# A two-layer decoder trunk on one core: two of seven activation blocks of the last MLP's down pairs kept in DRAM as high and low parts

## What is computed

```python
h = _modulate(_rmsnorm(x, norm_g[layer, 1]), sh2, sc2)
y = jnp.square(jax.nn.relu(h @ mlp_w_up[layer])) @ mlp_w_down[layer]
x = x + g2[:, None, :] * y
```

## Time and profile before

| | us |
|---|---|
| median of 3 runs | 2564.92 (2563.69 to 2565.44) |
| the profiled execution | 2562.76 |
| its span | 2561.0 |
| PE busy | 2484.8 (97%) |
| DVE busy | 1712.5 (67%) |
| ACT busy | 1041.6 (41%) |
| up pairs of the last MLP | about 1945 to 2212 of the span |
| down pairs | about 2258 to 2508 |
| last plain units | about 2511 to 2557 |

### The profile page before, as it was taken

How to read it: one execution, slowest core, us unless ns; L and a number is a source line. 1 busy time by engine, 2 the same in 40 slices (tenths; PEclk the granted TensorE clock), 3 DMA queues, 4 the chain that set the end, 5 groups by cost and what they waited for, 6 DMA issues and landing times. The chain is left out here.

```text
span 2561.0 us, 33801 instructions
## 1 busy us (share of the span) xinstructions
PE 2484.8 (97%) x12076; PEld 2028.1 (79%) x12076; DVE 1712.5 (67%) x2132; ACT 1041.6 (41%) x1486; POOL 149.1 (6%) x155
## 2 busy tenths in 40 slices
PE   6999999999999999999999999999999999998998
PEld 4888888888888878888898887666788888877877
DVE  6878776668876666666633545777259777588873
ACT  5553342236445431111311335777326544434321
POOL 0000000000000000000000003666000000000000
PEclk9999999999999999999999999999999999999999
DMA  6335573213444475553142364554333444734412
GB/s 256 128 136 185 192 261 117 99 58 125 163 160 152 172 272 187 186 206 135 48 151 75 112 176 136 127 128 107 123 115 107 144 158 149 270 113 151 175 43 111
DMA packets 135898, 378.54 MB, mean 148 GB/s; under 512 B 12656, under 2 KB 29040, under 8 KB 131824
## 3 DMA queue, kind: packets, MB, share of 16 engines
q1 hardware_dynamic: 135792, 377.11, 43.2%
HBM read 279.54 MB, written 97.52 MB: 147 GB/s over the span
## 5 line engine op out<-in xcount | busy, mean ns | idle before, releaser
L2435 PE MATMUL PS<-H_HI,W_HI 128*128 128x512 f32 x700 | 277.1, 396 | 3.3 <-DVE H_LO L1643 2.2
L2437 PE MATMUL PS<-H_HI,W_LO 128*128 128x512 f32 x700 | 272.9, 390 | 0.0
L2436 PE MATMUL PS<-H_LO,W_HI 128*128 128x512 f32 x700 | 272.6, 389 | 0.0
L2435 PE MATMUL PS<-HID_HI,W_HI 128*128 128x512 f32 x640 | 251.3, 393 | 7.2 <-DVE HID_LO L1869 3.3
L411 ACT ACTIVATE W_HI<-RAW 128x1024 fp32r<-128x1024 f32 x90 | 93.9, 1057 | 386.4 <-PE PS L2437 292.0
L2437 PE MATMUL PS<-HID_HI,W_LO 128*128 128x512 f32 x640 | 249.7, 390 | 0.0
L2436 PE MATMUL PS<-HID_LO,W_HI 128*128 128x512 f32 x640 | 249.7, 390 | 0.0
L1699 DVE SCALAR_TENSOR_TENSOR X<-PS,MODV,X 128x1024 f32<-128x1024 f32 x76 | 97.4, 1282 | 145.6 <-PE PS L2437 138.3
L2356 DVE TENSOR_TENSOR_SCAN KEEP<-PS,MASK 128x1024 f32<-128x1024 f32 (+3 forms) x112 | 147.6, 1349 | 46.9 <-ACT PS L1520 37.6
L2435 PEld LDWEIGHTS PS<-H_HI,W_HI 128*128 128x128 f32 x700 | 131.5, 188 | 32.9 <-DVE H_LO L1643 4.2
L2437 PEld LDWEIGHTS PS<-H_HI,W_LO 128*128 128x128 f32 x700 | 131.4, 188 | 28.3
(11 more groups left out here) (270 smaller groups left out, 5811.7 us busy)
## 6 DMA issues: line engine op xcount, KB each, us to landing
RAW<-in_wt SPq DMA_DIRECT2D x184, 512.0 KB, 4.1
MODRAW<-in_modw SPq DMA_DIRECT2D x96, 512.0 KB, 3.3
B_RAW<-block_scratch SPq DMA_DIRECT2D x21, 1024.0 KB, 8.0
hid_scratch<-TN SPq DMA_DIRECT2D x66, 256.0 KB, 2.2
HRAW<-hid_scratch SPq DMA_DIRECT2D x8, 2048.0 KB, 8.6
hid_scratch<-SCR SPq DMA_DIRECT2D x60, 256.0 KB, 2.2
x_scratch<-X SPq DMA_DIRECT2D x3, 4096.0 KB, 13.4
X<-x_scratch SPq DMA_DIRECT2D x6, 2048.0 KB, 8.7
```

The lines of the kernel that those rows point to most:

```text
L2435: pe.matmul(dst, w_hi, m_hi, start=first, stop=False)
L2436: pe.matmul(dst, w_hi, m_lo, start=False, stop=False)
L2437: return pe.matmul(dst, w_lo, m_hi, start=False, stop=last)
```

## The change

In the up pairs, N3 and N4 are cut as soon as their differences are made: ACT copies TD3 and TD4 into unused places of the weight ring (`down_hi`, before the first `finish` of the pair), DVE subtracts (`down_lo`, between the cut of S4 and `c12`), in place. SP stores four blocks for the two (`store_cut`, behind the first store of a pair), and N1 and N2 as before. The DRAM scratch has nine blocks a pair instead of seven. In the down pairs, `load_block` loads N3 and N4 twice, straight into B_HI and B_LO; their `b_hi` on ACT and `b_lo` on DVE are gone, and PE's product waits for the DMAs instead. In the last down pair DVE makes one of the four HID_LO before the addition of M22's bank and three behind it, where it made all four before. The diff, with the declarations of the new semaphores (`td_hi`, `td_lo`) and changes of counts left out where they only renumber:

```diff
@@ -37,7 +37,8 @@
...
 DPAIRS = 3 * GROUP_PAIRS
-M11, N1, N2, M21, N3, M22, N4 = range(PRODUCTS)
+M11, N1, N2, M21, N3, M22, N4, N3_HI, N4_HI = range(PRODUCTS + 2)
+CUT_HERE = PRODUCTS - 2
 W1, W2, WA, W3, W4, WD = range(BLOCKS)
...
@@ -298,6 +299,8 @@
...
                               enumerate((RC, RC + 2 * KB, RX + 28 * KB, RX + 30 * KB))]
+        TD3_HI, TD4_HI = W_HI[:, 4:8, 3 * P:4 * P], W_LO[:, 4:8, 3 * P:4 * P]
+        TD3_LO, TD4_LO = [at(f"TD_LO{n}", [P, HALF], F32R, off) for n, off in ((3, RC + 2 * KB), (4, RX + 30 * KB))]
         WX_HI = at("WX_HI", [P, 8, 3 * P], F32R, RX)
...
@@ -589,16 +592,22 @@
...
                 def store_sums(p, x):
-                    to = {n: BD[(p + DPAIRS * n).v] for n in (N1, N2, N3, N4)}
-                    made = [(p * 4 + n).v for n in range(1, 5)]
+                    to = {n: BD[(p + DPAIRS * n).v] for n in (N1, N2)}
+                    made = [(p * 4 + n).v for n in (1, 3)]
                     sp.wait_ge(sem["td_made"], made[0])
...
                     sp.wait_ge(sem["td_made"], made[1])
-                    sp.dma_start(to[N3], TD3[:]).then_inc(sem["td_out"], 16)
-                    sp.wait_ge(sem["td_made"], made[2])
                     sp.dma_start(to[N2], TD2[:]).then_inc(sem["td_out"], 16)
-                    sp.wait_ge(sem["td_made"], made[3])
-                    sp.dma_start(to[N4], TD4[:]).then_inc(sem["td_out"], 16)
+
+                def store_cut(p):
+                    to = {n: BD[(p + DPAIRS * n).v] for n in (N3_HI, N4_HI, N3, N4)}
+                    made = [(p * 2 + n).v for n in (1, 2)]
+                    sp.wait_ge(sem["td_lo"], made[0])
+                    sp.dma_start(fours(to[N3_HI]), TD3_HI.bitcast(F32)).then_inc(sem["td_out"], 16)
+                    sp.dma_start(to[N3], TD3_LO[:].bitcast(F32)).then_inc(sem["td_out"], 16)
+                    sp.wait_ge(sem["td_lo"], made[1])
+                    sp.dma_start(fours(to[N4_HI]), TD4_HI.bitcast(F32)).then_inc(sem["td_out"], 16)
+                    sp.dma_start(to[N4], TD4_LO[:].bitcast(F32)).then_inc(sem["td_out"], 16)
 
...
@@ -614,6 +623,8 @@
...
                         load_mod(sp, p // 2 * 3 + GMODS + 2)
+                    if sums:
+                        store_cut(p - 1)
                     store(p, 2, 0, 1, 1)
...
@@ -696,7 +707,12 @@
...
                     a = DPAIRS * b + GROUP_PAIRS * g
-                    sp.dma_start(B_RAW[b][:], BD[a:a + GROUP_PAIRS].rearrange("j p s -> p j s")
+                    if b in (N3, N4):
+                        h = DPAIRS * (N3_HI if b == N3 else N4_HI) + GROUP_PAIRS * g
+                        sp.dma_start(B_HI[b][:].bitcast(F32), BD[h:h + GROUP_PAIRS].rearrange("j p s -> p j s")
+                                     ).then_inc(sem[f"b_in{b}"], 16)
+                    to = B_LO[b][:].bitcast(F32) if b in (N3, N4) else B_RAW[b][:]
+                    sp.dma_start(to, BD[a:a + GROUP_PAIRS].rearrange("j p s -> p j s")
                                  ).then_inc(sem[f"b_in{b}"], 16)
...
@@ -720,7 +736,7 @@
...
                     sp.wait_ge(sem[f"hs_out{b}"], 64 * (PAIRS // 2) * 2 + 64 * 6)
-                sp.wait_ge(sem["td_out"], 16 * 3 * DPAIRS)
+                sp.wait_ge(sem["td_out"], 16 * 5 * DPAIRS)
                 sp.wait_ge(sem["product"], count_of(2, p, PRODUCTS, 7).v)
...
@@ -1218,6 +1234,8 @@
...
                         block_cut(p + 1, 1 - x, b)
+                    if m == 2 and (p.i is not None or p.c):
+                        down_hi(p - 1)
                     if stat:
...
@@ -1227,6 +1245,14 @@
...
                             act.activation(V_TOT[:], V_SPREAD, ACT.Copy).then_inc(sem["v_kept"], 1)
+
+                def down_hi(p):
+                    if p.i is not None or p.c:
+                        act.wait_ge(sem["td_out"], (p * 80).v)
+                    act.wait_ge(sem["td_made"], (p * 4 + 2).v)
+                    act.activation(TD3_HI, fours(TD3[:]), ACT.Copy).then_inc(sem["td_hi"], 1)
+                    act.wait_ge(sem["td_made"], (p * 4 + 4).v)
+                    act.activation(TD4_HI, fours(TD4[:]), ACT.Copy).then_inc(sem["td_hi"], 1)
 
...
@@ -1321,7 +1347,7 @@
...
                     else:
-                        act.wait_ge(sem["td_out"], 16 * 3 * DPAIRS)
+                        act.wait_ge(sem["td_out"], 16 * 5 * DPAIRS)
                         act.wait_ge(sem["hs_out1"], 64 * (PAIRS // 2) * 2 + 64 * 6)
...
@@ -1333,7 +1359,6 @@
...
                 b_hi(M21, 0)
-                b_hi(N3, 0)
                 d_hi(0, W3)
...
@@ -1347,16 +1372,12 @@
...
                     d_hi(q + 1, W1)
-                    if j == 0 and g:
-                        b_hi(N3, g)
                     d_hi(q + 1, W2)
...
                         b_hi(M11, g + 1)
-                    if j == 0:
-                        b_hi(N4, g)
                     d_hi(q + 1, W3)
...
@@ -1831,7 +1852,7 @@
...
                                     if (p.c - 1) % 2 == 0 else ((p - 2) // 2 * 64 + 64 * (PAIRS // 2) * m + 64).v)
-                        dve.wait_ge(sem["td_out"], (p * 48).v)
+                        dve.wait_ge(sem["td_out"], (p * 80).v)
                     else:
...
@@ -1840,6 +1861,14 @@
...
                     dve.tensor_tensor(TD4[:], c21, TD2[:], ALU.subtract).then_inc(sem["td_made"], 1)
+
+                def down_lo(p):
+                    dve.wait_ge(sem["td_hi"], (p * 2 + 1).v)
+                    dve.tensor_tensor(fours(TD3_LO[:]), fours(TD3[:]), TD3_HI.bitcast(F32), ALU.subtract
+                                      ).then_inc(sem["td_lo"], 1)
+                    dve.wait_ge(sem["td_hi"], (p * 2 + 2).v)
+                    dve.tensor_tensor(fours(TD4_LO[:]), fours(TD4[:]), TD4_HI.bitcast(F32), ALU.subtract
+                                      ).then_inc(sem["td_lo"], 1)
 
...
@@ -1911,6 +1940,8 @@
...
                     block_cut(p + 1, 1 - x, S4)
+                    if m == 2:
+                        down_lo(p - 1)
                     if kind == "v":
...
@@ -2094,7 +2125,6 @@
...
                 b_lo(M21, 3)
-                b_lo(N3, 4)
                 d_lo(0, W3)
...
@@ -2104,7 +2134,7 @@
...
                     refill = j == GROUP_PAIRS - 1 and not last
-                    cut = PRODUCTS * g
+                    cut = CUT_HERE * g
                     d_lo(q, WD)
...
@@ -2116,8 +2146,6 @@
...
                         d_lo(q + 1, W1)
-                    if j == 0 and g:
-                        b_lo(N3, cut + 4)
                     done(q, 2)
...
@@ -2125,7 +2153,7 @@
...
                     if j == 0:
-                        b_lo(M22, cut + 5)
+                        b_lo(M22, cut + 4)
                     done(q, 3)
...
@@ -2135,26 +2163,26 @@
...
                     dve.tensor_tensor(D_KEPT[:], bank(N3), D_KEPT[:], ALU.add).then_inc(sem["d_add"], 1)
-                    if j == 0:
-                        b_lo(N4, cut + 6)
                     to_x(q, 7, D_KEPT[:], 1, 1)
...
                         cut_lo(dve, Count(t0 + UPS + 5))
-                        for i in range(4):
-                            hid_lo(Count(1), i, 1, HRAW[1])
+                        hid_lo(Count(1), 0, 1, HRAW[1])
                     if refill:
-                        b_lo(M11, cut + 7)
+                        b_lo(M11, cut + 5)
                     if not last:
...
                     to_x(q, 6, bank(M22), 0, 1)
+                    if last:
+                        for i in range(1, 4):
+                            hid_lo(Count(1), i, 1, HRAW[1])
                     if refill:
-                        b_lo(N1, cut + 8)
+                        b_lo(N1, cut + 6)
                     if not last:
...
                     if refill:
-                        b_lo(N2, cut + 9)
+                        b_lo(N2, cut + 7)
                     done(q, 6)
...
@@ -2783,7 +2811,10 @@
...
                     pe.wait_ge(sem["d_lo"], BLOCKS * q + w + 1)
-                    pe.wait_ge(sem["b_lo"], PRODUCTS * (q // GROUP_PAIRS) + n + 1)
+                    if n in (N3, N4):
+                        pe.wait_ge(sem[f"b_in{n}"], 32 * (q // GROUP_PAIRS) + 32)
+                    else:
+                        pe.wait_ge(sem["b_lo"], CUT_HERE * (q // GROUP_PAIRS) + (M11, N1, N2, M21, M22).index(n) + 1)
                     if q:
...
                     w_hi, w_lo = d_place(W_HI, w), d_place(W_LO, w)

...
```

More of the change, by code:

```diff
@@ L214, in build @@
             a_ok at_full at_kept o_hi o_lo x_back_hi
-            td_made td_out b_in0 b_in1 b_in2 b_in3 b_in4 b_in5 b_in6 d_in0 d_in1 b_hi b_lo d_hi d_lo d_sum d_prod d_kept d_add
+            td_made td_hi td_lo td_out b_in0 b_in1 b_in2 b_in3 b_in4 b_in5 b_in6 d_in0 d_in1 b_hi b_lo d_hi d_lo d_sum d_prod d_kept d_add
             t_sum t_hi t_lo r_made relu_made pl_out0 pl_out1 w_sum product s_kept c_made h_made hs_out0 hs_out1 hr_in0 hr_in1 xm_lo xm_hi
@@ L371, in build @@
         HIDD = nc.dram_tensor("hid_scratch", [UPS, P, S], F32).ap()
```

(2 more changed lines are left out.)

## The result

The changed kernel took 2551.14 us (median of 6 runs, 2548.47 to 2552.59) against 2563.53 of the kernel before (6 runs, 2561.92 to 2565.44): a ratio of 0.9949, 95% interval 0.9937 to 0.9962, 12.4 us less. The prediction had reckoned from a median of 2564.92 and forecast 15.4 us less. The profiled execution has a span of 2550.7.

The account below looks back on a forecast made before the run. PE was taken as the bound everywhere except one pair at each boundary, where DVE is. −3.89 − 4.87 − 4.77 − 3.6 = −17.1, + 1.7 for one clock loss, −15.4: 2549.5 us, range 2546.5 to 2555.

Parts of the forecast that it names:

- case with two clock losses: Forecast time if both new waits before M22 bring a half-clock loss: 2551.3 us.
- q=0: First down pair: without N4's low part, N4 starts when M22's matmuls end; 3.89 us gained.
- q=4 and q=8: First down pairs of groups 1 and 2: M22's low part late next, wait 3.0 us; 4.87 and 4.77 gained.
- Clock: Half-clock matmuls behind the two new 3.0 us waits before M22: 0.6 chance each, likeliest one loss, +1.7 us.
- The last pair: End of the down pairs: one HID_LO, M22's addition, then three; waits under 0.6 us each, 3.6 gained.
- Loads: Boundaries, ten loads for eight: low parts of N3 and N4 land 10.4 and 13.2 us after issue; price nothing.
- first rival: Late loads of N3 and N4 stop PE 5 us at two boundaries: 2559.5; 0.14, shared with partial boundary gain.
- Up pairs: Added copies, subtractions and stores fit in idle time; DVE idle before c21 near 0.2; price 0, bounds 0 to 1 us.
- second rival: Up pairs: stores in 512 B pieces delay DVE if landing exceeds 7.7 us; 2570 us at 14.3; chance 0.03.
- third rival: Waits called "issue" not for B_LO, so q=4 and q=8 keep most loss: 2557.4 or 2559; chance 0.04.

Follow-up runs that it names:

- e1: The changed kernel timed again with no edit; 2549.28 us, ratio 0.9942 to the kernel before.
- e5: The changed kernel with eight extra matmuls on PE ahead of M22 in q=4 and q=8; 2545.96 us, ratio 0.9928 to the kernel before.
- e6: The changed kernel with only N3 cut in the up pairs, N4 cut in the down pairs as before; 2556.3 us, ratio 0.9966 to the kernel before.
- e7: The changed kernel without the up pairs' copy, subtraction and extra stores, uncut N3 and N4 loaded twice (output wrong); 2549.51 us, ratio 0.9938.
- e3: The kernel before with only the last down pair's order changed (one HID_LO, M22's addition, three HID_LO); 2560.31 us, ratio 0.9986.
- e4: The changed kernel with only N4 cut in the up pairs, N3 cut in the down pairs as before; 2552.22 us, ratio 0.9955 to the kernel before.
- e8: e2 plus two DVE reorders: N4's addition before W4's low part at group ends, two HID_LO before M22's addition in the last pair; 2540.04 us, ratio 0.9897.
- e2: The changed kernel with M22's high part (ACT) and low part (DVE) made earlier in q=4 and q=8; 2539.79 us, ratio 0.9903 to the kernel before.

## Why the prediction was right, and where its sizes were off

The range (2546.5 to 2555.0) held 2551.14, and the way and the mechanism were right. The forecast of 2549.5 was 1.6 us too low, but as a gain it was off by more: 15.4 forecast, 12.4 measured, since the kernel before came out 1.4 faster than the median that the prediction started from. The traces give 14.1 to 14.2, so 1.3 of the 3.0 is the sum's own error, a second clock loss that it left out. The other 1.7 lies within the scatter of the medians: the interval of the ratio reaches from about 10 to 16 us, and the same kernel gave 14.7 in e1. That 2551.14 lies on the 2551.3 of the case with two clock losses is in part luck.

**q=0: right.** −3.89 forecast, −3.9 in every trace whose N4 comes cut.

**q=4 and q=8: right, with the clock counted once too few.** M22's low part is late next, as the step said: the wait is 2.85 printed, 3.0 with the 0.16. In the trace with the clock loss taken away (e5) the two boundaries gain 4.9 and 4.9, where the prediction had 4.87 and 4.77; e5 leaves the end of DVE's work where it was.

**Clock: the mis-sized term.** I gave each new wait 0.6 and put one loss of 1.7 in the sum. The runs show two losses of 1.5 to 1.6. All eight waits of 2.85 or so before M22 in the four kernels that have them (the changed kernel, e1, e6, e7) were followed by half clock. The two waits of 3.66 at q=4 and q=8 of before led me to think it a coin; in e3 and e4 the same waits were followed by half clock at both places. With two, the sum is 17.1 − 3.1 = 14.0, and the traces show 14.1 to 14.2. That a wait of this length must be followed by half clock is still not shown. In e8 PE waited 2.89 near 942 us, and the clock behind it stayed full (PE's timeline, then PE by windows, e8_order):

```profile
942.13 0.47 PE L2470 MATMUL PS<-HID_HI,W_HI 128*128 128x512 f32 x1 [2.89 <-DVE X L1722]
942.00:946.00 4.00, 3.87 (x17) 1.00 0.43 136
```

**The last pair: right.** −3.6 forecast, −3.6 to −3.7 in the traces, −3.6 in the medians of e3. The three waits are three times 0.15 to 0.18.

**Loads: right.** PE waited for no DMA from 2100 us on. ACT's waits for B_RAW were 16.0 us, against 15.5 before, off the path that PE's time takes. Loads between 2320 and 2350 us, after (count, KB, median us to landing):

```profile
B_RAW<-block_scratch SPq DMA_DIRECT2D x5, 1024.0 KB, 7.7
B_HI<-block_scratch SPq DMA_DIRECT2D x2, 1024.0 KB, 9.2
B_LO<-block_scratch SPq DMA_DIRECT2D x2, 1024.0 KB, 11.8
```

The forecast had 10.4 and 13.2 for the low parts of N3 and N4. The view of the tile B_LO between 2300 and 2400 us parts the 11.8 into the two:

```profile
DMA to landing us min/median/max: 10.5/11.8/13.1
```

Both are met to 0.1 us. The first rival did not happen.

**Up pairs: right, and shown twice.** DVE rests 0.19 before c21 (forecast: near 0.2), and ACT 0.39 before its copy; ACT's timeline, after:

```profile
2123.92 0.60 ACT L1190 ACTIVATE TN<-PS 128x512 f32<-128x512 f32 x1 [0.39 <-PE PS L2465]
```

e7 shows no price of the added work. The second rival asked how the stores in pieces of 512 B land. After, in the up pairs:

```profile
block_scratch<-TD_LO SPq DMA_DIRECT2D x24, 256.0 KB, 2.7
...
block_scratch<-W_HI SPq DMA_DIRECT2D x12, 256.0 KB, 2.7
block_scratch<-W_LO SPq DMA_DIRECT2D x12, 256.0 KB, 2.8
```

The high parts (W_HI and W_LO here, the ring places they lie in) land in 2.7 and 2.8 us, like the low parts in pieces of 2 KB. The rival's threshold was 7.7. The Trainium skill, page "DMA: Bandwidth & Descriptors", section "Specifications", has 512 B as the smallest piece at full rate; the trace agrees, with 2.7 and 2.8 us against 2.7. The TD stores of N1 and N2, issued right behind the next two loads of weights as before, still land in 5.2, so the 5.3 from which the rival reckoned seems to go with that place in SP's queue; no run moved them. The rival's prices don't add up as written: with its own 12.2 us and 11 us for each further one, the gain of 15.4 would be gone at 13.6 and not 13.8, and 14.3 would give about 2573 and not 2570. Nothing else hung on them.

**The third rival** (the waits called "issue" are not for B_LO) is excluded by the place of the new wait, 0.1 us behind the end of M22's low part, and by e2.

**What the sum could not see** is the state in which an execution reaches the last MLP: 0.6 us early to 6.6 us late in ten traces, while the part that the change touches repeats to 0.1. The changed kernel's two medians, 12.4 and 14.7 us below before, lie on both sides of the 14.1 of its traces. That the lateness is chance and not a trait of a kernel is shown for one kernel with two executions; what starts it, at 937, in the attention or elsewhere, was not tried and stays open.

## What to carry to other kernels

When an engine is the bound only at a boundary, list its queue there in order and ask of each item what is late next. Here taking two of seven long items out left M22's late, and moving that one item forward was worth another 9 us. Count a wait together with the clock that can go with it: a rest of 3 us cost 4.6, and eight matmuls without a use in the rest bought 1.6 of it back. And before a median is set against a sum, measure from the last landmark that both kernels share.

## What the runs showed of the hardware

- Behind each of the eight waits of 2.84 to 2.87 us before M22 PE's granted clock was 0.50, 1.2 GHz, which cost the changed kernel 1.5 to 1.6 us each time; with eight matmuls in the wait and 1.02 us of rest left it stayed at 1.00 (e5). It was also half behind N4's wait of 2.04 in q=0 in the three kernels that have it (before, e3, e6), and stayed full behind waits of 1.57 (e6), 1.83 (e7) and 2.89 (e8) near 940 us. So the length of the wait alone doesn't settle it. Of the waits of 3.66 and 3.67 before N3, in three kernels, five of six were followed by half clock and one was not.
- A half clock and a late DVE hide each other: in e4 the slow N3 took away M22's wait, in e6 the slow M22 took 1.6 of N4's at q=4 and all of it at q=8.
- Stores of 256 KB out of SBUF in pieces of 512 B landed as fast (2.7 to 2.8 us) as in pieces of 2 KB (2.7).
